# Two pairs of output column groups with seven block products each, and their weight sums on GpSimd

## The reference, cut to what matters

```python
h = rmsnorm(x, norm_g)                       # x: 1 x 256 x 2048
z = h @ w_in                                 # 2048 x 6144, split into eight parts
q_a, k_a, v_a, g_a, u_p, g_p, q_m, g_m = split(z)
y_a = causal_attention(q_a, k_a, v_a) * silu(g_a)        # 8 heads of 128
y_p = multiscale_pool(u_p, w_pool, pool_scale) * silu(g_p)
y_m = memory_attention(q_m, mk, mv) * silu(g_m)          # mk, mv = split(rmsnorm(mem) @ w_mem_kv)
y = concat([y_a, y_p, y_m]) @ w_out          # 256 x 2048 times 2048 x 2048
out = rmsnorm(x + y, final_norm_g)
```

## Time and profile before

| | before |
|---|---|
| runs, median of 3 (lowest to highest) | 429.95 us (429.71 to 430.3) |
| span of the profiled execution | 427.9 us |
| PE busy, share of the span | 419.0 us, 98% |
| DVE busy | 303.5 us, 71% |
| ACT busy | 241.6 us, 56% |
| POOL busy | 39.5 us, 9% |
| first matmul of `OUT0` | 335.82 us |
| last matmul starts | 420.12 us |

### The profile page before, as it was taken

The page is one execution under the profiler, slowest core; times in us unless marked ns, Lnnn a source line. Parts: engine busy times, 40 slices in busy tenths (PEclk is TensorE's granted clock), DMA queues, the critical chain, the costliest instruction groups (busy, mean ns, idle before and its releaser), DMA issues.

```text
span 427.9 us, 5921 instructions
## 1 busy us (share of the span) xinstructions
PE 419.0 (98%) x2244; PEld 361.4 (84%) x2244; DVE 303.5 (71%) x330; ACT 241.6 (56%) x325; POOL 39.5 (9%) x64
## 2 busy tenths in 40 slices
PE   8999999999999999999999999999999999999993
PEld 7888888888888888888888888888899888888882
DVE  4875865456786699857466878877667488897842
ACT  6764784474363766464465446555565566765611
POOL 1000000000050000000000232302000201000160
PEclk9999999999999999999999999999999999999998
DMA  8999959998989528746336256465646999567023
GB/s 284 415 414 420 404 202 376 121 337 309 163 198 298 192 97 310 224 156 196 100 114 231 98 178 215 150 196 162 231 149 214 241 387 290 197 247 294 0 88 108
DMA packets 28251, 96.34 MB, mean 225 GB/s; under 512 B 3776, under 2 KB 4288, under 8 KB 27328
## 3 DMA queue, kind: packets, MB, share of 16 engines
q1 hardware_dynamic: 24624, 83.26, 57.4%
q0 software_dynamic: 1152, 4.19, 5.5%
q10 hardware_dynamic: 2448, 8.52, 5.5%
HBM read 93.87 MB, written 2.10 MB: 224 GB/s over the span
## 4 chain that ended last, share of the span: by engine, by line
PE 94%; issue 2%; DVE 1%; DMA 1%; DVEq 0%; POOLq 0%; POOL 0%; ACT 0%
PE ps L622 36%; PE ps L625 18%; PE ps L640 4%; PE ps L638 4%; PE ps L639 4%; PE ps L681 3%; PE ps L679 3%; PE ps L680 3%; PE ps L662 3%; PE ps L664 3%; PE ps L663 3%; PE ps L603 3%; PE ps L610 1%; DMA mem_raw<-in_mem_head 1%; PE ps L716 1%
## 5 line engine op out<-in xcount | busy, mean ns | idle before, releaser
L1098 DVE TENSOR_TENSOR w_lo<-w_raw,w_hi 128x1024 fp32r<-128x1024 f32 x133 | 165.7, 1262 | 72.9 <-ACT w_hi L863 72.4
L622 PE MATMUL ps<-xT,w_hi 128*128 128x512 f32 x640 | 201.9, 397 | 0.0
L863 ACT ACTIVATE w_hi<-w_raw 128x1024 fp32r<-128x1024 f32 x133 | 138.2, 1056 | 83.1 <-PE ps L625 49.5
L625 PEld LDWEIGHTS ps<-xT,w_lo 128*128 128x128 f32 x640 | 120.2, 188 | 28.4
L625 PE MATMUL ps<-xT,w_lo 128*128 128x256 f32 x640 | 125.8, 278 | 0.0
L622 PEld LDWEIGHTS ps<-xT,w_hi 128*128 128x128 f32 x640 | 97.8, 189 | 0.3
L975 ACT ACTIVATE part_b<-ps 128x1024 f32<-128x1024 f32 x11 | 11.3, 1026 | 18.2 <-PE ps L625 18.2
L639 PE MATMUL ps<-w_lo,yT 128*128 128x512 f32 x46 | 17.9, 389 | 0.0
L638 PE MATMUL ps<-w_hi,yT 128*128 128x512 f32 x46 | 17.9, 389 | 0.0
L640 PE MATMUL ps<-w_hi,yT 128*128 128x512 f32 x46 | 17.9, 389 | 0.0
L863 ACT ACTIVATE w_hi<-x_f 128x1024 fp32r<-128x1024 f32 x8 | 8.5, 1061 | 10.5 <-PE ps L681 5.1
(11 more groups left out here) (207 smaller groups left out, 622.1 us busy)
## 6 DMA issues: line engine op xcount, KB each, us to landing
w_raw<-in_w_in SPq DMA_DIRECT2D x94, 512.0 KB, 4.5
w_raw<-in_w_out SPq DMA_DIRECT2D x30, 512.0 KB, 5.2
w_raw<-in_w_mem_kv SPq DMA_DIRECT2D x13, 512.0 KB, 12.4
x_t_raw<-in_x_t SPq DMA_DIRECT2D x8, 256.0 KB, 13.1
rows<-in_x ACTq DMA_DIRECT2D x2, 1024.0 KB, 10.2
rows<-in_mem ACTq DMA_DIRECT2D x2, 1024.0 KB, 11.4
x_f<-in_w_in SPq DMA_DIRECT2D x4, 512.0 KB, 6.9
x_f<-in_w_in POOLq DMA_DIRECT2D x4, 512.0 KB, 11.1
```

Of the source, the lines that this page charges most:

```text
L622: pe.matmul(ps[:, bank0(g) + f, :], hi[:, t, f * P:(f + 1) * P], moving[:, kt], start=(kt == 0), stop=(kt == KT - 1), skip_group_check=True)
L625: m = pe.matmul(ps[:, bank0(g) + f, 0:S], lo[:, t, f * P:(f + 1) * P], moving[:, kt, 0], start=False, stop=(kt == KT - 1), skip_group_chec ...
L863: act.activation(halves_of(n)[0], whole_of(n), ACT.Copy).then_inc(hi_done, 1)
L1098: dve.tensor_tensor(lo, whole_of(n), hi.bitcast(F32), ALU.subtract).then_inc(lo_done, 1)
```

## The change

The plain group `OUT0` and the plain group `LAST` disappear. There are two pairs, `OUT0` with `OUT1` and `OUT2` with `LAST`, each with 14 block products and 8 plain units, in orders of their own. The right sides f4 to f7 of both pairs are made by POOL as tensor additions, 16 of them; the first three stand ahead of the gate product of the third branch. The block B11 is loaded by SP into `f5_a` or `f5_b`, and the adding transfers of the output are gone; those of the pair of value groups stay. The finish of the last gate, which lay in the units of `OUT0`, moves into the first pair. The values pair and everything ahead of `GM` are the same.

```diff
-PAIRS = ((V0, V1), (OUT1, OUT2))
+def output_units(one, two):
+    return ((M2, 0), (M2, 1), (N5, 0), (N5, 1), (M3, 0), (one, 4), (M6, 0), (M1, 0), (one, 5), (M6, 1), (M1, 1),
+            (M3, 1), (one, 6))
+PAIRS = ((V0, V1), (OUT0, OUT1), (OUT2, LAST))
+OUT_UNITS = (output_units(OUT0, OUT1) + ((M4, 0), (M4, 1), (OUT0, 7), (OUT1, 4), (N7, 0), (OUT1, 5), (OUT1, 6),
+                                         (N7, 1), (OUT1, 7)),
+             output_units(OUT2, LAST) + ((LAST, 4), (LAST, 5), (OUT2, 7), (LAST, 6), (LAST, 7), (M4, 0), (M4, 1),
+                                         (N7, 0), (N7, 1)))
+OUT_SUMS = ((N5, 0), (N5, 1), (M1, 0), (M1, 1), (M4, 0), (M4, 1), (N7, 0), (N7, 1))
+SUMS_AHEAD = 3
...
+            def output_sum(q, g, i):
+                f5 = f5_of(q)
+                if g == N5:
+                    pool.wait_ge(f5_landed[q - 1][i], 16)
+                    b12 = piece_landed(q, M2, i)
+                    if q == 1:
+                        pool.wait_ge(pv_done, 2 * len(JOBS))
+                    else:
+                        pool.wait_ge(lo_done, unit_in(1, N5, i) + 1)
+                    out, left, right = f4[:, i], f5[:, i], b12
...
+                pool.tensor_tensor(out, left, right, ALU.add).then_inc(f_summed, 1)
...
                 if g == MEM_JOB:
-                    for k in range(BLOCKS):
-                        pool.wait_ge(f4_landed[1][k], 16)
-                        pool.dma_start(f4[:, k], out_w_dram[OUT1 - OUT0, 2 * k], accum_op=ALU.add
-                                       ).then_inc(f4_summed[1][k], 16)
+                    for f in OUT_SUMS[:SUMS_AHEAD]:
+                        output_sum(1, *f)
                 pool.wait_ge(gate_tanh, i + 1)
...
+            for f in OUT_SUMS[SUMS_AHEAD:]:
+                output_sum(1, *f)
+            for f in OUT_SUMS:
+                output_sum(2, *f)
...
+            for h in range(TH):
+                for g in (OUT0, OUT1):
+                    weigh(g, h, 4)
+            weigh(OUT2, 0, 5)
+            weigh(OUT2, 1, 7)
             for h in range(TH):
                 pool.wait_ge(ms2_ready, h + 1)
                 pool.tensor_tensor(rstd[:, h:h + 1], ms[:, h:h + 1], power[:, 0:1], ALU.pow).then_inc(rstd2_ready, 1)
...
+                elif n >= PAIR:
+                    act.wait_ge(f_summed, output_sums_done(pair_of(n), g, i))
...
+            act.wait_ge(pv_done, 2 * len(JOBS))
+            for h in range(TH):
+                act.dma_start(x_res[:, h], x_dram[h]).then_inc(res_landed, 16)
             for n in range(PAIR, UNITS):
...
+            dve.wait_ge(res_landed, 16 * TH)
             for n in range(PAIR, UNITS):
                 for m in pieces_to_split(n):
                     split_lo(m)
...
+            mean_of(0, 6)
+            dve.wait_ge(piece_used, unit_in(2, M4, 1) + 1)
+            add_last(1, bank0(LAST) + 1, before_end, ALU.subtract).then_inc(summed, 1)
+            settle(add_last(1, bank0(LAST) + 1, end))
+            finish(0, 5)
+            dve.wait_ge(half_used, 1)
+            add_last(1, LAST_N7, end).then_inc(summed, 1)
...
+            mean_of(1, 9)
+            finish(1, 6)
```

More of the change, by code:

```diff
@@ L1064, in _ @@
                                   ).then_inc(fg_landed, 16)
-                if unit(n) == (OUT2, 5):
-                    squares_of(OUT1)
-                if n == LAST_UNIT:
-                    squares_of(OUT2)
-            for h in range(TH):
-                if h == 0:
-                    act.wait_ge(summed, LAST - OUT0 + 1)
-                    square_sum(0, end, LAST - OUT0)
-                else:
-                    for i, part in enumerate(LAST_PARTS):
-                        act.wait_ge(summed, LAST - OUT0 + 2 + i)
-                        square_sum(1, slice(end.start + part.start, end.start + part.stop), LAST - OUT0 + i)
+                if n == PAIR + 18:
+                    act.wait_ge(summed, 1)
+                    for h in range(TH):
+                        square_sum(h, columns_of(OUT0), 0)
@@ new lines, in _, with scale_end @@
+                if n == PAIR_B + 2:
+                    act.wait_ge(summed, 2)
+                    for h in range(TH):
+                        square_sum(h, columns_of(OUT1), 1)
+                if n == PAIR_B + 16:
+                    act.wait_ge(summed, 3)
+                    square_sum(0, columns_of(OUT2), 2)
+            act.wait_ge(summed, 4)
+            square_sum(0, end, 3)
+            act.wait_ge(summed, 5)
+            square_sum(1, columns_of(OUT2), 2)
+            def scale_end(h):
@@ L1082, in _ @@
                 act.dma_start(out_dram[h, :, end], end_scaled[:, h]).then_inc(stored, 16)
+            scale_end(0)
+            for i, part in enumerate(LAST_PARTS):
+                act.wait_ge(summed, 6 + i)
+                square_sum(1, slice(end.start + part.start, end.start + part.stop), 3 + i)
+            scale_end(1)
         @block.vector
@@ L1419, in _ @@
-            dve.wait_ge(sq_done, TH * (LAST - OUT0))
-            settle(dve.tensor_reduce(sst[:, :], ssq[:, :, 0:LAST - OUT0], AX.X, ALU.add))
-            settle(dve.tensor_scalar(sst[:, :], sst[:, :], EPS, None, ALU.add))
-            def add_last(h, bank, part):
-                c = slice(end.start + part.start, end.start + part.stop)
-                dve.tensor_tensor(x_res[:, h, c], ps[:, bank, part], x_res[:, h, c], ALU.add).then_inc(summed, 1)
+                    add_products(OUT0).then_inc(summed, 1)
@@ L1427, in weigh_last, with add_last @@
+            def add_last(h, bank, c, left=ALU.add):
+                return dve.tensor_tensor(x_res[:, h, c], x_res[:, h, c], ps[:, bank, c.start % COLS:(c.stop - 1) % COLS + 1],
+                                         left)
             def weigh_last(h, part):
```

446 lines of the change are left out of this document (241 added, 205 removed).

## The result

| | before | changed |
|---|---|---|
| median of the runs (lowest to highest) | 429.95 us (429.71 to 430.30, 3 runs) | 459.78 us (458.66 to 461.16, 4 runs) |
| ratio, 95% interval | | 1.069 (1.0656 to 1.0724) |
| profiled execution: time, span | span 427.9 us | 460.81 us, span 459.0 us |
| last matmul ends | 420.40 us | 447.53 us |
| DVE's last scaling ends | 423.69 us | 454.77 us |

A fourth run of the kernel before took 708.41 us; it stands apart from all others and is left out. The change is 29.8 us slower; 460.2 us was forecast, 30.2 more. The busy shares of the changed kernel, which answer to the earlier trace rows, hide where it went: PE has 12 matmuls less and is 5.9 us longer busy, POOL works 45 us more.

What follows compares the result with a forecast made beforehand. It took PE to bound the output before the change and the port shared by DVE and POOL after it; terms from -2.7 to +12.5 sum to +30.2, on 429.95 giving 460.2 us, range 450 to 467 us.

Steps and rivals of the forecast that it cites:

- 12 matmuls fewer: Output: 360 matmuls of 512 columns instead of 372, at 0.2267 us each, -2.7 us.
- entry, copies behind POOL's first sum: Before the first pair: ACT's attention copies stand behind its split of POOL's first sum, so PE starts later, +1.9 us.
- fourth unit (N5, 1): First pair: its split comes late behind POOL's sums and DVE's product with `x_rstd`, so PE waits, +1.8 us.
- residual ahead of (M3, 0): First pair: DVE makes no split until the late load of `x_res` lands, so PE waits, +8.5 us (4.5 to 13).
- rest of the first pair's sums: After the wait for `x_res`, about two remaining POOL sums meet DVE's splits, +3.5 us (0 to 5).
- second pair's sums: Eight POOL sums in a chain, each letting one DVE instruction through: 27.5 us against 15.0 of PE work, +12.5 us.
- weighing: Five of six weighings move ahead of the last matmul, covered by units of 2.72 us, +0.7 us (0 to 3).
- the end: Last matmul to last scaling: POOL's first root stands behind a weighing and DVE's `finish(0)` waits for it, +4.0 us.
- The first rival: Splits run on beside POOL's sums, so the shared port's terms go: +12.5, 442.5 us, chance 0.09.
- The rival of a colder PE: After the long stall PE's clock falls to 1.2 GHz, some 16 matmuls cost twice: +3.6, 463.8 us, chance 0.25.
- The count for the whole stage: From the first pair's start, the shared port is wanted 93.5 us, PE 81.6; port bound, 9 us over before.

Runs made afterwards that it cites:

- the run with fills: Changed kernel with each of POOL's 16 output sums replaced by three fills that read nothing from SBUF, products using constants: 444.95 us.
- the second series: The changed kernel itself, unedited, run again on the same chip as the kernels with idle products on PE: 459.38 us.
- the last version: Changed kernel with sums moved to adding transfers and DVE, waits and order edited, last gate's product earlier and its tanh later: 436.86 us.
- that with 19 products: Changed kernel with 19 idle products of 128 columns on PE in the wait for the residual, ahead of the pair's fifth unit: 458.94 us.

## Why the prediction was right, point by point

The terms are read from the profiled execution; what PE lost is the time from one matmul's start to the next beyond 0.23 us, where that is over 0.12 us.

| term | predicted | measured |
|---|---|---|
| 12 matmuls fewer | -2.7 | -2.7 (2232 matmuls for 2244) |
| entry, copies behind POOL's first sum | +1.9 | +2.0 |
| fourth unit (N5, 1) | +1.8 | +1.5 |
| residual ahead of (M3, 0) | +8.5 | +8.9 |
| rest of the first pair's sums | +3.5 | +3.3, of it 0.5 waiting and the rest matmuls at half clock |
| second pair's sums | +12.5 | +10.0, and 1.7 at half clock behind them |
| weighing | +0.7 | no gap; 0.4 waiting for an ACT copy |
| the end | +4.0 | +3.95 (7.24 against 3.29) |

These come to 29 of the 31.1 us by which the span grew; the rest lies in pieces too small for this list. The residual's own numbers (350.9 + 1.2 + 1.2 - 345.0) give 8.3, not quite the 8.5 that the sum takes.

That the forecast is met within half a microsecond is partly luck. The 2.5 us too much for the second pair's sums are offset by 1.7 us at half clock and 2 us of small pieces that the sum does not have, and the runs of the changed kernel alone lie 3.4 us apart. The row of the first pair's remaining sums agrees in number and not in kind: waits for splits were predicted, and it is mostly slow matmuls. With the clock held up the waits show, as 1.9 and 0.4 us.

The mechanism was right: the exclusion seen four times in the trace of before, 2.3 us a sum and one split between two sums, is what the second pair shows, and the run with fills, of the same length and behind the same waits, takes 15 us away. The first rival, splits that pass POOL, has fallen with its 442.5 us.

The step whose size was off most is "12.5 for the second pair's sums". The chain itself was sized well: it runs from 372.98 to 400.16 us, 27.2 against the 27.5 predicted. But PE got more work out of it: its gaps in the chain sum to 10.0, because PE began with a unit in hand, which the text had named only as a bound.

The step that was wrong in kind is the sum's silent assumption that the first pair's terms are separate. Each was there in the trace within 0.4 us. But removing the 8.9 us of the residual brought 1.4 to 1.8 us, removing the 2.0 us of the entry nothing, and keeping the clock up about 1.1. The four terms are largely one bill, six sums and a gate product that must pass between the splits, and the wait for the load is where it is paid. The load is a second bill that falls due in the same time (5.8 or 8.4 us where the sums do not meet the splits). The prediction had the pieces (sums made during that wait "cost nothing while DVE waits anyway") without turning them round: without the wait, they would cost.

The rival of a colder PE came half true: the clock did fall, to 0.50 from 352 to 360 us and again from 402 to 404. The prediction charged it 3.6 us. In the first pair the half speed was hidden behind the splits; the 1.7 us behind the second pair's last gap, behind which the next wait is 0.4 us for a copy on ACT, are in the time, as far as the trace shows it; no run took that stretch alone away.

The count for the whole stage (93.5 us of wants on the port against 81.6 of PE) gave the sign and only 9 of 30 us. The likely reason, which no run tested by another number of slots, is that four slots of halves can't store what DVE could do in its free time elsewhere, so a chain of sums is paid where it runs.

Still open: the runs of the changed kernel lie from 457.9 to 461.3 us, and its two profiled executions differ in where the second pair's turns fall (waits of up to 2.25 us spread over the chain in the first, one of 4.1 us at 392 us in the second series; three of the edited kernels have one of 4.2 us near 390). What decides between them was not tried.

## What to carry to other kernels

When two engines exclude each other, price an instruction that is moved between them by what it holds up, not by its duration or by who waits for its result: eight additions that nobody needed cost 17.5 us here, some 5 of them by the clock that fell in the waits. And before the terms of a sum are added, ask for each wait what else is being paid while it lasts; a wait that covers another bill is worth little when it is removed. A saving of 2.7 us leaves no room for a new wait: sums where they are free (transfers, the engine that splits anyway) and an end as short as before had both to be there; the last version came near the first, with 4.7 us of small waits left, and missed the second.

## What the runs showed of the hardware that was not expected

A fill on POOL (1.97 us for two of 128x1024) leaves a split beside it at 1.22 us, an addition with two inputs takes it to 3.4, and a scaling with one input mostly leaves it at 1.2 and holds a few up by 0.84 us. The Trainium skill, page "SBUF — State Buffer", section "SBUF: two separate sides", says that the pair of SBUF ports that DVE and GpSimd share is held for the whole instruction by whichever starts first, a DVE instruction with two SBUF inputs included. The additions agree. The one-input scalings, of 3.3 us, which hold a split up by 0.84 us, do not.

The clock: behind the gap of 8.8 us PE's granted clock stayed at 0.50 from its restart at 354.28 until about 360.4 us, though it was working nearly all that time; with idle products up to the end of the gap it did not fall there. Products that ended 4.5 us ahead of the restart did not prevent it. A short wait can be followed by half clock too: behind the entry's wait of 2.0 to 2.1 us the granted clock from 338 to 342 us is 1.00 in the first profile of the changed kernel, 0.57 in the run with fills and 0.58 in that with 19 products. What decides was not tried.
